# A hybrid mLSTM and S5 decoder layer on one core: a reordered opening, early sample states, and half of the step-input table built by GpSimd

## The reference

```
h    = rmsnorm(x, g_mix)                      # 1024 wide
q, k, v, o, ig, fg, u, gl = split(h @ w_in + b_in)
lf   = log_sigmoid(fg)
hA   = mlstm(q, k, v, ig, lf, C0, n0, m0)     # 4 heads of 256; exact causal, max-stabilised
yA   = (sigmoid(o) * rmsnorm(hA) * g_hn) @ w_a
abar = exp(dt * (A_re + i A_im));  bbar = (abar - 1) / A * B
s    = associative_scan(abar, bbar @ u)       # 32 groups of 16 channels, 64 complex states each
yS   = gelu(Re(C s) + D u);  yB = (yS * sigmoid(yS @ w_glu + b_glu)) @ w_b
x    = x + (sigmoid(gA) * yA + sigmoid(gB) * yB) @ w_out
x    = x + (silu(hf @ w_ff1) * (hf @ w_ff3)) @ w_ff2      # hf = rmsnorm(x, g_ffn)
y    = rmsnorm(x, g_final)
```

## Time and profile before

| | us |
|---|---|
| median of 3 runs | 1031.87 (1030.63 to 1032.9) |
| the profiled execution, its own time | 1032.94 |
| its span, first to last instruction | 1031.0 |
| TensorE busy | 976.4 (95%) |
| VectorE busy | 567.1 (55%) |
| ScalarE busy | 419.8 (41%) |
| GpSimd busy | 189.1 (18%) |

### The profile page before, as it was taken

One profiled execution on the slowest core, in us unless ns is written; L12 is line 12 of the kernel. 1 busy time (PEld: TensorE's weight loads), 2 busy tenths in 40 slices (PEclk: granted clock), 3 DMA queues, 4 the chain that ended last, 5 costly groups with the idle time before them and its releaser, 6 DMA issues.

```text
span 1031.0 us, 19911 instructions
## 1 busy us (share of the span) xinstructions
PE 976.4 (95%) x8196; PEld 933.5 (91%) x8196; DVE 567.1 (55%) x936; ACT 419.8 (41%) x625; POOL 189.1 (18%) x346
## 2 busy tenths in 40 slices
PE   4896989999999999889999999999999999999994
PEld 3895779899889989789999999999999999999994
DVE  6799586388358449475333465544445444432334
ACT  5422726743672492552323344333333333222221
POOL 3197852454184103100000000000000000000000
PEclk9998999999999999899999999999999999999997
DMA  6232416227323423334243322323232323233312
GB/s 257 65 103 75 175 42 255 77 74 253 100 94 128 171 103 132 113 123 172 96 123 103 103 82 82 103 82 101 81 102 81 101 82 99 84 103 102 102 41 83
DMA packets 27172, 114.67 MB, mean 111 GB/s; under 512 B 3332, under 2 KB 3380, under 8 KB 25192
## 3 DMA queue, kind: packets, MB, share of 16 engines
q1 hardware_dynamic: 21744, 79.21, 24.1%
q0 software_dynamic: 2992, 25.43, 6.5%
q10 hardware_dynamic: 2376, 9.17, 2.3%
HBM read 100.40 MB, written 13.40 MB: 110 GB/s over the span
## 4 chain that ended last, share of the span: by engine, by line
PE 90%; DVE 7%; ACT 1%; issue 1%; DMA 1%; DVEq 0%; SPq 0%; ACTq 0%
PE G L1414 69%; PE G L1488 4%; PE Q L1414 2%; PE Q L1495 2%; PE Q L1536 2%; PE G L1576 1%; PE Q L1523 1%; PE Q L1533 1%; PE G L1567 1%; PE Q L1499 1%; DVE c_samples L1195 1%; PE Q L1625 1%; PE G L1568 1%; PE Q L1452 1%; PE Q L1596 1%
## 5 line engine op out<-in xcount | busy, mean ns | idle before, releaser
L411 ACT ACTIVATE w_high<-raw 128x1024 fp32r<-128x1024 f32 (+1 forms) x147 | 155.4, 1058 | 351.1 <-PE G L1414 309.3
L1414 PE MATMUL G<-h_high,w_high 128*128 128x256 f32 x1360 | 278.1, 286 | 13.7 <-DVE v_samples L1149 9.1
L936 DVE TENSOR_TENSOR w_low<-raw,w_high 128x1024 fp32r<-128x1024 f32 x146 | 181.2, 1241 | 178.0 <-ACT w_high L411 177.2
L1414 PE MATMUL G<-h_low,w_high 128*128 128x256 f32 x1360 | 275.5, 284 | 0.0
L1414 PE MATMUL G<-h_high,w_low 128*128 128x256 f32 x1360 | 275.4, 284 | 0.0
L1414 PEld LDWEIGHTS G<-h_high,w_high 128*128 128x128 f32 x1360 | 212.6, 190 | 16.3 <-DVE v_samples L1149 9.3
L1414 PEld LDWEIGHTS G<-h_low,w_high 128*128 128x128 f32 x1360 | 212.7, 190 | 0.0
L1414 PEld LDWEIGHTS G<-h_high,w_low 128*128 128x128 f32 x1360 | 212.3, 190 | 0.0
L1414 PE MATMUL G<-hidden_high,w_low 128*128 128x256 f32 x352 | 70.9, 282 | 0.0
L1414 PE MATMUL G<-hidden_low,w_high 128*128 128x256 f32 x352 | 70.8, 282 | 0.0
L1414 PE MATMUL G<-hidden_high,w_high 128*128 128x256 f32 x352 | 70.6, 282 | 0.0
(11 more groups left out here) (368 smaller groups left out, 1567.6 us busy)
## 6 DMA issues: line engine op xcount, KB each, us to landing
raw<-wst SPq DMA_DIRECT2D x147, 512.0 KB, 3.5
c_samples<-c POOLq DMA_DIRECT2D x4, 2048.0 KB, 9.0
out_cs<-c_samples POOLq DMA_DIRECT2D x4, 2048.0 KB, 7.5
v_spread<-v_scratch ACTq DMA_DIRECT2D x4, 1024.0 KB, 4.7
x_tokens<-xt SPq DMA_DIRECT2D x4, 520.0 KB, 6.0
x_residual<-xt POOLq DMA_DIRECT2D x1, 2080.0 KB, 8.4
out_y<-x_residual ACTq DMA_DIRECT2D x8, 260.0 KB, 2.2
small<-small ACTq DMA_DIRECT2D x1, 1785.0 KB, 8.6
```

Source lines behind the costliest of these rows:

```text
L411: return act.activation(out, in_, ACT.Copy, **kw)
L936: tt(WL[n.slot()][:], raw[n.slot()][:], WH[n.slot()][:].bitcast(F32), ALU.subtract).then_inc(w_lo, 1)
L1414: last = mm(o, w[slot][:, c], h[:, k, c0_:c0_ + width], start=start and x == 0 and t == 0, stop=stop and x == n - 1 and t == 2)
```

## The change

Four things are done at once.

- The opening. TensorE multiplies each piece of the first half with unit 2 (k0) too, as it comes. ScalarE rounds unit 2 before the first piece, loads the table for Sqrt with a dummy instruction, and takes the two Sin instructions out of the middle of the first half to its end; the 1.8 MB load `small` is issued later. VectorE inverts the second half before `low` of unit 2. The units of q move to other PSUM banks (q0 to B, q1 to the first pair of Q), so other semaphores guard them (`u_ready`, `k0_ready`; `rows_in` guards the value tiles instead of q0).
- VectorE's list. The powers of `abar` come first, with `low` of units 3 and 4 between them, then k0 and the gate rows, then k1, then the parameters of the scan, and only then the gate chain. The parameters are squared six times in 24 instructions (51 with the writing before), and written in one piece per head: 24 instructions of 4 or 24 elements per partition.
- The sample states of head 0. `load_cs(0)` is issued when the last piece of x has been scaled (the gate rows no longer lie in that tile's place), and `scale_cs` of head 0 stands before ScalarE's wait for the first o unit.
- The step table. In heads 1 to 3 ScalarE writes blocks 0 and 1 only; GpSimd writes blocks 2 and 3 (`spread_half`, 16 instructions) of the next head's table after `x_done`, before it spreads u. TensorE waits for a further semaphore, `baq_pool`.

```diff
@@ ScalarE, opening
                 act.activation(x_sq[:, k, :], X[:, k, :], ACT.Square).then_inc(sq_ready, 1)
-                if k == 3:
+                if k == 1:
                     act.wait_ge(par_in, 16)
                     act.activation(par[:, 2, :], par[:, 2, :], ACT.Exp).then_inc(s5_dt, 1)
-                if k == 6:
-                    act.dma_start(sm[:], small[:, 0:NSM]).then_inc(sm_in, 16)
             act.wait_ge(s5_arg, 1)
             act.activation(tp[0][:], tp[0][:], ACT.Exp).then_inc(s5_mag, 1)
+            act.wait_ge(consts, 1)
+            act.activation(junk_a[:], eps[:], ACT.Sqrt)
...
+            act.dma_start(sm[:], small[:, 0:NSM]).then_inc(sm_in, 16)
             high(At(1))
+            high(At(2))
...
@@ ScalarE, a head
                     act.wait_ge(x_done, h)
                     spread(0)
-                    spread(1)
+                    spread(1).then_inc(baq_act, 1)
...
-                if h >= 1:
-                    spread(2)
                 after(n.plus(6))
-                if h >= 1:
-                    spread(3).then_inc(baq_act, 1)
                 act.wait_ge(v_ready, h + 1)
                 act.dma_start(v_scr, vS[P - NS:P, :]).then_inc(vs_out, 16)
-                if h >= 1:
+                if h == 0:
+                    scale_cs()
+                else:
                     gelu(h - 1)
...
-                if h == 0:
-                    scale_cs()
@@ GpSimd
+            def spread_half(h):
+
+                for q in (2, 3):
+                    for jj in range(PAIRS):
+                        for g in range(2):
+                            last = pool.tensor_scalar(BAQ[32 * q:32 * q + 32, jj, :, :, 64 * g:64 * g + 64], step_rows(jj, q),
+                                                      parity[32 * jj:32 * jj + 32, g:g + 1], None, ALU.mult)
+                            if q == 2 or jj < PAIRS - 1 or g == 0:
+                                own.do(last)
+                last.then_inc(baq_pool, 1)
+                pool.wait_ge(baq_pool, h)
...
                     pool.wait_ge(x_done, h + 1)
+                    spread_half(h + 1)
                     spread_uq(h + 1)
...
             load_vb(0)
+            guard(xg_ready, 2 * KC)
+            load_cs(0)
             pool.wait_ge(uq_clear, 1)
             spread_uq(0)
@@ VectorE, the scan's parameters (now before fln)
+            pre, pim = a_pow[:, 0, 2, 256:272], a_pow[:, 1, 2, 256:272]
+            for lev in range(LEVELS):
+                qre, qim = tp[0][:, 16 * lev:16 * lev + 16], tp[1][:, 16 * lev:16 * lev + 16]
+                own.add(tt(tp[0][:, 128:144], pre, pre, ALU.mult))
+                own.add(tt(tp[1][:, 128:144], pim, pim, ALU.mult))
+                own.do(stt(qim, pre, 2.0, pim, ALU.mult, ALU.mult))
+                own.do(tt(qre, tp[0][:, 128:144], tp[1][:, 128:144], ALU.subtract))
+                pre, pim = qre, qim
...
+                for h in range(H):
+                    own.add(dve.tensor_copy(par_of(h, name_re).rearrange("p (l j) -> p l j", j=PAIRS), re[:, h]))
+                    own.add(ts(to_im[:, h, :, 0, :], im[:, h], -1.0, None, ALU.mult))
+                    own.add(dve.tensor_copy(to_im[:, h, :, 1, :], im[:, h]))
...
             dve.wait_ge(fln, 1)
-            own.do(tt(lf[:], lf[:], gt[4][:], ALU.subtract))
+            own.do(tt(lf[:], lf[:], gt[2][:], ALU.subtract))
@@ TensorE, opening
-                    for t, h in enumerate((HH, HL)):
-                        mm(G[:, B + half, 0:w], WH[1][:, P * k:P * k + P], h[:, k, c], start=k == 0 and t == 0, stop=False)
+                    for u, out in ((1, G[:, B + half, 0:w]),) + (((2, Q[:, half, 0:w]),) if half == 0 else ()):
+                        if half == 0 and k == 0:
+                            pe.wait_ge(w_hi, u + 1)
+                        for t, h in enumerate((HH, HL)):
+                            mm(out, WH[u][:, P * k:P * k + P], h[:, k, c], start=k == 0 and t == 0, stop=False)
...
             unit(At(N_MIX + 2), HH, HL, 6)
-            pe.wait_ge(rows_in, 1)
-            unit(At(N_MIX + 3), HH, HL, A)
             pe.wait_ge(u_ready, 1)
-            unit(At(N_MIX + 4), HH, HL, B)
+            unit(At(N_MIX + 3), HH, HL, B)
+            pe.wait_ge(k0_ready, 1)
+            unit(At(N_MIX + 4), HH, HL, 4)
```

More of the change, by code:

```diff
@@ L1008, in _ @@
-            h_low(2 * KC - 1)
-            dve.wait_ge(sm_in, 16)
-            dve.tensor_copy(hp[:, :, 0:10], smv("hp").rearrange("p (h c) -> p h c", h=H)).then_inc(hp_ready, 1)
-            low(At(RING))
-            done(At(0))
-            bg = smv("b_gate")
-            ig, fg, ab, lf, cum, on4, mx = gt[0], gt[1], gt[2], gt[5], gt[6], gt[7], gt[8]
-            for c0_, w in HALVES:
-                bank = A + (c0_ > 0)
-                own.add(ts(ig[:, c0_:c0_ + w], G[0:4, bank, 0:w], bg[0:4, 0:1], None, ALU.add))
-                own.add(ts(fg[:, c0_:c0_ + w], G[32:36, bank, 0:w], bg[32:36, 1:2], None, ALU.add))
@@ L1020, in _ @@
-            own.settle()
-            stt(ab[:], fg[:], -1.0, fg[:], ALU.mult, ALU.max).then_inc(rows_in, 1)
-            own.add(dve.memset(on4[:], 1.0))
-            own.do(ts(lf[:], fg[:], 0.0, None, ALU.min))
-            low(At(N_MIX + RING))
             def take_u(h):
@@ L1052, in k_or_q, with tsc @@
                 low(n.plus(1 + j + RING))
-            k_or_q(0, 0)
+            own.add(dve.memset(ones[:], 1.0))
+            dve.memset(half_pi[:], 1.5707963267948966)
+            dve.memset(eps[:], EPS).then_inc(consts, 1)
+            dve.memset(UQ[:], 0.0).then_inc(uq_clear, 1)
+            def tsc(o, a, s1, op1, s2=None, op2=ALU.bypass):
+                own.do(ts(o, a, s1, s2, op1, op2) if s2 is not None else ts(o, a, s1, None, op1))
+            ai, dt = par[:, 1, :], par[:, 2, :]
+            t = [x[:] for x in tp]
@@ new lines, in add_squares @@
+            def add_squares(p):
+                dve.wait_ge(sq_ready, 2 * p + 2)
+                tt(x_sq[:, 2 * p, :], x_sq[:, 2 * p, :], x_sq[:, 2 * p + 1, :], ALU.add).then_inc(sq_added, 1)
+            C1, C2 = 6.28125, 4058.0 / 2 ** 21
+            C3 = 6.283185307179586476925 - C1 - C2
+            ROUND = 1.5 * 2 ** 23
+            add_squares(0)
+            dve.wait_ge(s5_dt, 1)
+            own.do(tt(t[1], dt, ai, ALU.mult))
+            tsc(t[4], t[1], 0.15915494309189535, ALU.mult)
@@ new lines, in _ @@
+            tsc(t[4], t[4], ROUND, ALU.add)
+            tsc(t[4], t[4], -ROUND, ALU.add)
+            add_squares(1)
+            for c in (C1, C2, C3):
+                own.do(stt(t[1], t[4], -c, t[1], ALU.mult, ALU.add))
+            add_squares(2)
+            add_squares(3)
+            tsc(t[1], t[1], 3.1415925, ALU.min, -3.1415925, ALU.max)
+            stt(t[3], t[1], -1.0, t[1], ALU.mult, ALU.max).then_inc(s5_ang, 1)
+            dve.wait_ge(w_hi, 1)
+            gate_cols = lambda ap: ap.rearrange("p (k c) -> p k c", c=P)[:, :, 0:64]
@@ new lines, in _, with invert, h_low @@
+            tt(gate_cols(WL[0][:]), gate_cols(raw[0][:]), gate_cols(WH[0][:].bitcast(F32)), ALU.subtract).then_inc(w_lo, 1)
+            def invert(half):
+                c0_, w = HALVES[half]
+                dve.wait_ge(rx_root, half + 1)
+                own.do(dve.reciprocal(rx[:, c0_:c0_ + w], rx[:, c0_:c0_ + w]))
+            def h_low(i):
+                k, (c0_, w) = i % KC, HALVES[i // KC]
+                dve.wait_ge(hh_ready, i + 1)
+                tt(HL[:, k, c0_:c0_ + w], xg[k % 2][:, c0_:c0_ + w], HH[:, k, c0_:c0_ + w].bitcast(F32), ALU.subtract).then_inc(hl_ready, 1)
@@ new lines, in _ @@
+            invert(0)
+            dve.wait_ge(gb_in, 16)
+            for i in range(2 * KC):
+                k, (c0_, w) = i % KC, HALVES[i // KC]
+                if i == 5:
+                    low(At(1))
+                if i == KC:
+                    h_low(i - 1)
+                    invert(1)
+                    low(At(2))
+                if i >= 2:
+                    dve.wait_ge(hl_ready, i - 1)
+                stt(xg[k % 2][:, c0_:c0_ + w], X[:, k, c0_:c0_ + w], g_mix[:, k:k + 1], rx[:, c0_:c0_ + w], ALU.mult, ALU.mult).then_inc(xg_ready, 1)
+                if i not in (0, KC):
+                    h_low(i - 1)
@@ L1069, in _ @@
             credit(pow_ready)
+            low(At(N_MIX + RING))
             dve.wait_ge(s5_den, 1)
             dve.reciprocal(tp[2][:], tp[2][:]).then_inc(s5_rden, 1)
-            k_or_q(0, 1)
+            k_or_q(0, 0)
+            done(At(0))
+            bg = smv("b_gate")
+            ig, fg, ab, lf, cum, mx = gt[0], gt[1], gt[2], gt[3], gt[4], gt[1]
+            for c0_, w in HALVES:
+                bank = A + (c0_ > 0)
+                own.add(ts(ig[:, c0_:c0_ + w], G[0:4, bank, 0:w], bg[0:4, 0:1], None, ALU.add))
+                own.add(ts(fg[:, c0_:c0_ + w], G[32:36, bank, 0:w], bg[32:36, 1:2], None, ALU.add))
```

145 lines of the change are left out of this document (47 added, 98 removed).

## The result

The changed kernel took 1025.90 us, the median of 5 runs (1025.51 to 1028.13), against 1031.87 us; the ratio is 0.9947 with a 95% interval of 0.9928 to 0.9965. Its profiled execution has a span of 1025.5 us and took 1027.24. Forecast were 1023.4 us and a range of 1017.0 to 1029.5: faster, as said, and 2.5 us less so.

The account below looks back on a forecast made before the run. TensorE was taken as the bound, so gains come only where it stands still: -2.8 us in the opening and -5.7 in head 0's middle, 8.5 off the median 1031.87, giving 1023.4; range 1017.0 to 1029.5.

Parts of the forecast that it names:

- The opening's start and the seam: Between the halves: 37 matmuls fewer, some 4 us, TensorE at the value tiles at about 60 instead of 64.1.
- the sign: At the value tiles: TensorE waits 10 to 13 us for `w_low`, and not at all for the value rows.
- The new wait for ScalarE's rounding behind the ln: Before `low` of unit 6: VectorE idles 2 us because ScalarE rounds that unit behind the log-sigmoid.
- The 48 small instructions: Scan parameters on VectorE's opening list: 0.224 us each, 10.8 us in all, ending at 67.1.
- the dense price: Rival for the small instructions: 0.32 us each, 15.2 us, 4.4 us later, total 1027.8; chance 0.14.
- the tiles' start: Value tiles in the opening: start at 72.1 us, not at 65.21, with TensorE idle some 12 us before them.
- Scores and value rows: Before head 0's o unit: scores end at 94.6 with 2.3 us clock loss, value rows some 2 us earlier.
- the first place: Opening up to head 0's first o unit, with its 9.1 us wait for the value rows: -2.8 us.
- The sample states: Middle of head 0: updates end about 12 us earlier, waits of 1.1 and 2.9 us and half clock go, -5.7 us.
- The step table: Heads 1 to 3: GpSimd gains 16 instructions per head at 0.8 us, 13 us a head, with no loss.
- The slower rival: Heads 1 and 2: GpSimd's spread holds VectorE, kernel slower from 0.63 us delay each, 1040.8 at full price; chance 0.11.
- my correction of the level: From span to median: profiled execution 1.07 us above the median, so 8.5 taken off 1031.87, giving 1023.4.

Follow-up runs that it names:

- e11: The changed kernel with ScalarE's rounding of the value tiles' first chunk ahead of its exp and ln of the gate rows: 1023.13 us, ratio 0.9911.
- e10: The changed kernel with GpSimd's work on the input factors held until VectorE's 48 small instructions are through: 1020.97 us, ratio 0.9906.
- e9: The kernel before, unchanged, run and profiled again: 1032.58 us, ratio 1.0000, profiled span 1029.1.
- e2: The changed kernel with the second half of the step-input table back on ScalarE in heads 1 to 3: 1024.84 us, ratio 0.9930.
- e1: The changed kernel again, unchanged: 1025.17 us, ratio 0.9937 to the kernel before.
- e4: The kernel before with only the second half of the step-input table moved to GpSimd in heads 1 to 3: 1037.82 us, ratio 1.0054.
- e5: The changed kernel with head 0's sample states scaled late and the step table's second half on ScalarE, only the opening staying changed: 1031.48 us, ratio 0.9998.

## Why the prediction came out as it did

**The opening's start and the seam.** Forecast for the end of k1's copy were 53.0 us. It was 51.1: the last h_low ended at 36.4, not at 37.7, since the first half of h was also quicker at its start (TensorE waits once, 3.3 us, for the first piece, where four waits stood). TensorE was ready for the value tiles at 58.5, not at 60, and waited 14.3 us there, more than the 10 to 13 that I had named as the sign. The new wait for ScalarE's rounding behind the ln came as described, 1.86 us instead of 2, and e11 prices it.

**The 48 small instructions** are the mis-sized term: 10.8 us forecast, 14.3 measured, nearly the dense price. The step that failed is taking the mean of one mixed stretch. The earlier trace rows held the answer in its POOL column: in 84.55:91.50, with GpSimd busy 6.40 of 6.95 us, an instruction cost 0.32. e10 shows that GpSimd alone makes the difference (0.11 without it). The error was 3.5 us. That the tiles' start was met all the same, 72.8 for 72.1, is luck: the list was 1.9 us ahead, and the chain behind the small instructions took 4.1 us, not 5.0.

**Scores and value rows.** The scores were to end at 94.6 with 2.3 us of clock loss and 2 us of slack for the value rows. They ended at 94.62; the tiles took 16.07 us, 1.6 over their full-clock time, and the value rows were there at 92.4. Against the first profile of the kernel before the first place gave -2.77 us for -2.8; against the second it is 2.2 (e9 stands at -0.54).

**The sample states.** -5.7 forecast; the lead grew by 5.74. The forecast that the updates would "follow at once" held (117.41 us, no idle time), but not their 7.23 us:

```profile
117.41 11.95 DVE L1209 SCALAR_TENSOR_TENSOR c_samples<-v_spread,sample_small,c_samples 128x256 f32<-128x256 f32 x16
135.41 1.19 DVE L964 TENSOR_SCALAR s_out<-G,head_params 128x256 f32<-128x256 f32 x2
```

Moved 15 us forward they fell into GpSimd's build of the next head's tables, each of whose two-operand instructions holds one update, as it holds the small ones above: at 118.02 us an update takes 1.50 us beside one of GpSimd's of 1.35. They took 11.95 us, and u was out at 136.6, 0.8 us before TensorE's next unit began at 137.4. The margin was nearly gone, and I had not counted it.

**The step table.** No loss in heads 1 to 3: right, by e2. Its price was not: 1.28 us an instruction, not 0.8. The slower rival (0.63 us of delay each) did not come, although the table and the updates do overlap in head 1, where the updates start 3 us sooner than with the table on ScalarE (205.82 us in e1, 208.84 in e2), as forecast. The two stretches of 16 updates, head 0's and head 1's, in the changed kernel, and below them head 0's in the kernel before:

```profile
117.41:129.36 11.95, 11.15 (x98) 10.08 (x98) 11.95 (x18) 2.92 (x9) 10.73 (x17) 1.00 0.16 45
205.65:213.13 7.48, 7.48 (x52) 7.03 (x52) 7.48 (x18) 1.38 (x4) 6.03 (x8) 1.00 0.26 71
```

```profile
132.22:139.45 7.23, 6.13 (x52) 5.92 (x50) 7.23 (x17) 2.12 (x2) 2.28 (x5) 1.00 0.01 2
```

Two neighbouring updates of head 1, and the table instruction beside the first of them:

```profile
210.02 0.69 DVE L1209 SCALAR_TENSOR_TENSOR c_samples<-v_spread,sample_small,c_samples 128x256 f32<-128x256 f32 x1
210.63 0.47 DVE L1209 SCALAR_TENSOR_TENSOR c_samples<-v_spread,sample_small,c_samples 128x256 f32<-128x256 f32 x1
209.97 0.92 POOL L843 TENSOR_SCALAR b_abar_by_step<-b_abar,parity 32x256 f32<-32x256 f32 x1
```

An update that nothing holds takes 0.47 us, and the next follows after 0.40, so sixteen would take some 6.4 us (an estimate from these rows). In head 0 of the changed kernel they take 5.5 us more, beside GpSimd's adds and multiplies of two operands. In head 1, beside five table instructions of 0.92 to 1.28 us with one operand each, five of the updates take 0.61 to 0.70 us, 0.14 to 0.23 more, and those between them 0.47. The Trainium skill (SBUF — State Buffer, the section "SBUF: two separate sides") has the later of the two wait for the whole of the other's instruction. The trace agrees for GpSimd's two-operand instructions and not for the table's. What I missed is e4: the price of the table depends on where the updates stand. The same small holds, 1.0 us over sixteen updates, lie on TensorE's path when the updates are late and off it when they are early. The two other edits took them out of its way; I had summed the three parts as if they were independent.

**From the profile to the median.** Here are the missing 2.5 us. By steps the sum was -8.5 and TensorE was 8.51 us ahead from head 0 to head 3; measured were -6.0 and, in e1's group, -6.6. 1.07 us of the 2.5 are my correction of the level. I took the 8.5 us off the median, though I had read them from an execution that took 1032.94; off that one they give 1024.4, and 1.5 us are missing. The differences, too, came from one execution of the kernel before, and e9 shows another that reaches head 0's sample sums 1.69 us sooner with nearly the same waits. What differs is how much of TensorE's work falls into half clock behind a wait. The 1.7 us that I booked as gained behind the wait for u are absent in e9. That the opening's share is the smallest follows from e5: 0.2 us by the ratio, 2.6 by the first profile, 0.7 by the second (1029.1 against 1028.4). How often each clock pattern occurs, and so how the 1.5 us divide between the two places, stays open.

## What to carry to other kernels

Price a run of small VectorE instructions by what GpSimd does beside them: count GpSimd's two-operand instructions, not VectorE's. Before a long helper task goes to another engine, look at what stands beside it once every other edit is in; the same move was free in one kernel and cost 5.6 us in the other. And take a clock loss behind a stall as a range from zero up, until a second profile of the same kernel shows it again.
